# Turning the first token tiles as they land, loading the small vectors from another queue, and spacing two prefix scans

## The chip, the cores and the metric

The kernel runs on one core of one Trainium2 chip, in one launch. A core has a matmul engine (TensorE, in the profile PE, with its weight loads as PEld), VectorE (DVE), ScalarE (ACT), GpSimd (POOL) and SyncE (SP), which issues most transfers. The engines run side by side and wait for each other by semaphores. The metric is the device time of one execution in microseconds (us). An execution under the profiler gives the trace from which the rows below are taken; its clock column is the TensorE clock that was granted, as a share of 2.4 GHz.

## What is computed

One inference step of a two-layer hybrid encoder in float32, for a prompt of 1024 tokens and for 8 running streams of 16 tokens each (1152 token rows of 1024 channels in all). Cut to what the change is near to:

```
h    = rms_norm(x, norm_mix[0])              # x: 1152 x 1024
proj = h @ w_in_ab                           # 1024 -> 2560: q, fz, i_in, g, p
log_f = logaddexp(log(lb), log1p(-lb) + log_sigmoid(fz))   # decays, 4 heads x 128
b    = cumsum(log_f)                         # inside a block of the recurrence
...  # chunked linear recurrence, pooling, output projection, gated FFN with causal conv
...  # layer 2: spatial-gating MLP over 128-token chunks, gated FFN; final rms_norm
```

The vectors `norm_mix`, `norm_ffn`, `hgrn_out_gain`, `pool_scale`, `c_ln_gain` and `c_ln_bias` are small: together 69 rows of 128 numbers.

## The kernel before

**Products.** A float32 matrix is split into a high part (rounded to the matmul format) and a low part (the rest), and a product is three matmuls, high by high, high by low and low by high: `xh`, `xl` hold the activations, `wh`, `wl` the weights. The tokens are cut into three blocks of 384 (`TB`), each of three tiles of 128. A weight piece is 128x512; it is loaded into one of four `raw` buffers by SyncE's queue, scaled on GpSimd by a gain out of `vec` (`scale_weights`, L2722), rounded on ScalarE (`high`, L2111) and its low part taken on VectorE (`low`, L1345). A unit of the first projection needs two pieces, 2j and 2j + 1, and yields one row block of 128 output channels for all tokens; its results are taken from PSUM by VectorE (`scaled`, L1362) into `work`.

**The start.** The tokens lie row by row in memory, and the matmuls want channels on the partitions. SyncE loads the nine token tiles into `xtok`, three to a block (`x_tiles`, L490), all three of a block counted on one semaphore. Behind the first block it loads the 69 vector rows into `vrow` (L499), then two weight pieces, then the second block and so on. TensorE turns a block in eight groups: `turn(g)` (L777) turns one slice of 128 channels of all three tiles into one PSUM bank, six banks in rotation, so that from the seventh group on it waits until VectorE is through with the bank. ScalarE makes `xh` of each group (`x_high`, L2150), VectorE makes `xl` (`x_part`, L1389). After the fourth group TensorE also turns `vrow` (L814), ScalarE copies the result to `vec` (L2168), and GpSimd, which builds masks and constants until then, waits for `vec` before its first `scale_weights`. ScalarE's first `high` and VectorE's first `low` stand in their programs behind all eight groups of the first block. Then TensorE starts the matmuls of the first unit on the first block (`block_of`, L792), and turns the second block, then the third, between its matmuls. The squares for the norm are taken on ScalarE in between (`x_squares`, L2157). The norm follows: `spread_norm` on TensorE (L806), a root on ScalarE (L2143), a reciprocal on VectorE (L1381), and only then are the first units taken from PSUM.

**The scans.** Units 0 to 3 yield `fz`. While units 4 to 8 run on TensorE, ScalarE and VectorE make the log decays out of it, beside the weights of the coming units. The last step is a prefix sum along the tokens for each of the four heads: `tensor_tensor_scan` over 1152 elements with `resetm` as a factor that is 0 at the start of each block (`decay`, L1449). In VectorE's loop over units (`for j in range(2, BESIDE)`) iteration j does `low(2j + 1)`, `low(2j + 2)` and the three `scaled` of unit j; two scans stand behind iteration 6 and two behind iteration 7. Each engine runs its program in the written order.

Of the kernel before, what the change touches and what calls it, by code (L numbers as in the profile page):

```python
# [20 lines left out]
ACT = mybir.ActivationFunctionType  # L21
ds = bass.ds

P = 128
# [7 lines left out]
KD = D // P  # L32
# [14 lines left out]
V_MIX, V_FFN, V_OUTG, V_PSC, V_LNG, V_LNB, NVEC = 0, 16, 32, 33, 37, 53, 69  # L47
# [35 lines left out]
def build(nc, A, O):  # L83
    ctx = ExitStack()
    with ctx:  # L85
        def sem(name):
            return ctx.enter_context(nc.semaphore(name))

        x_loaded = [sem(f"x_loaded{i}") for i in range(NTB)]
        rows_loaded = sem("rows_loaded")
        raw_loaded = [sem(f"raw_loaded{i}") for i in range(RAWS)]
# [21 lines left out]
        x_turned = sem("x_turned")  # L115
# [18 lines left out]
        vec_mm = sem("vec_mm")  # L134
        vec_ready = sem("vec_ready")
# [6 lines left out]
        logf_used = sem("logf_used")  # L142
        k_ready = sem("k_ready")
        reset_ready = sem("reset_ready")
        decay_ready = sem("decay_ready")
# [114 lines left out]
        work = at("work", [P, 24, TOK], F32, W0)  # L260
# [5 lines left out]
        ident = at("ident", [P, P], F32, ID0)  # L266
# [14 lines left out]
        TURN = (1, 2, 4, 5, 6, 7)  # L281
# [188 lines left out]
        def _(sp):  # L470
# [17 lines left out]
            def x_tiles(tb):  # L488
                for t in range(3 * tb, 3 * tb + 3):
                    sp.dma_start(xtok[:, t, :], xp[:, t, :] if t < NT - 1 else xsm).then_inc(x_loaded[tb], 16)  # L490
            x_tiles(0)
            rows = [(V_MIX, A["norm_mix"].rearrange("l (k p) -> (l k) p", p=P)),
                    (V_FFN, A["norm_ffn"].rearrange("l (k p) -> (l k) p", p=P)),
                    (V_OUTG, A["hgrn_out_gain"]),
                    (V_PSC, A["pool_scale"].rearrange("l (k p) -> (l k) p", p=P)),
                    (V_LNG, A["c_ln_gain"].rearrange("l (k p) -> (l k) p", p=P)),
                    (V_LNB, A["c_ln_bias"].rearrange("l (k p) -> (l k) p", p=P))]
            for r0, src in rows:
                sp.dma_start(vrow[r0:r0 + src.shape[0], :], src).then_inc(rows_loaded, 16)  # L499

            def unit_pieces(j):
                up(wab, 2 * j, 2 * j, UNITS[j] * P)
            unit_pieces(0)
# [166 lines left out]
        def _(pe):  # L670
# [98 lines left out]
            def turn(g):  # L769

                tb, d = divmod(g, KD)
                if d == 0:
                    pe.wait_ge(x_loaded[tb], 48)
                if g >= 6:
                    pe.wait_ge(xl_ready, g - 5)
                for j in range(3):
                    mm = pe.transpose(ps[TURN[g % 6]][:, j * P:(j + 1) * P], xtok[:, 3 * tb + j, d * P:(d + 1) * P],  # L777
                                      ident[:, :])
                mm.then_inc(x_turned, 1)
# [27 lines left out]
                                   start=True, stop=True)  # L807
                mm.then_inc(norm_mm, 1)

            for g in range(KD):  # L810
                turn(g)
                if g == 3:
                    pe.wait_ge(rows_loaded, 16 * 6)
                    pe.transpose(ps[3][:, 0:NVEC], vrow[:, :], ident[0:NVEC, 0:NVEC]).then_inc(vec_mm, 1)  # L814
            block_of(0, 0, lambda k: turn(KD + k))
            pe.wait_ge(vec_ready, 1)
            block_of(1, 0, lambda k: turn(2 * KD + k))
# [523 lines left out]
        def _(dve):  # L1341
            def low(n, s):

                dve.wait_ge(w_high_ready, n + 1)
                dve.tensor_tensor(wl[:, s % 2, :], raw[:, s % RAWS, :], wh[:, s % 2, :].bitcast(F32), ALU.subtract)\  # L1345
                    .then_inc(w_low_ready, 1)
# [95 lines left out]
                dve.wait_ge(logf_ready, c + 1)  # L1442
                dve.tensor_tensor(z, f, z, ALU.subtract).then_inc(logf_used, 1)

            def decay(c):
                dve.wait_ge(logf_used, c + 1)
                dve.wait_ge(reset_ready, 3)
                for h in (2 * c, 2 * c + 1):
                    dve.tensor_tensor_scan(work[:, 20 + h, :], resetm[:, :], work[:, 20 + h, :], 0.0,  # L1449
                                           ALU.mult, ALU.add).then_inc(decay_ready, 1)  # L1450

            for j in range(2, BESIDE):
                if j > 2:
                    low(2 * j + 1, 2 * j + 1)
                if j == 6:
                    log_keys(0)
                    log_keys(1)
                low(2 * j + 2, 2 * j + 2)
                for tb in range(NTB):
                    scaled(work[:, UNITS[j], tbs(tb)], g0 + 3 * j + tb, tb, t0 + 4 * j + 2 + tb)  # L1460
                if j == 5:
                    logf(0)
                    logf(1)
                if j in (6, 7):
                    decay(j - 6)

            def evict(j):
                for tb in range(NTB):
# [636 lines left out]
        def _(act):  # L2105
# [45 lines left out]

            def x_squares(t):

                act.wait_ge(x_loaded[t // 3], 48)
                if t:
                    act.wait_ge(x_squared, t)
                act.activation(xsq[:, :], xtok[:, t, :], ACT.Square, accum_out=sst[:, t:t + 1]).then_inc(x_squared, 1)  # L2157

            def high2(q):
                act.wait_ge(w_scaled, q + 3)  # L2160
                act.activation(wh2[:, q, :], raw[:, 2 + q, :], ACT.Copy).then_inc(w_high_ready, 1)

            n0, g0, t0 = PLAN.at["ab"]
            for g in range(KD):
                x_high(g)
                if g == 3:
                    act.wait_ge(vec_mm, 1)
                    act.activation(vec[:, 0:NVEC], ps[3][:, 0:NVEC], ACT.Copy).then_inc(vec_ready, 1)  # L2168
            high(0, 0, 0)
            high(1, 1, 0)  # L2170
            for k in range(KD):
# [825 lines left out]
```

## Time and profile before

| | us |
|---|---|
| median of 3 runs (lowest, highest) | 2929.57 (2926.86, 2929.97) |
| the profiled execution, its own time | 2928.97 |
| its span, first to last instruction | 2927.3 |
| TensorE busy | 2844.0, 97% of the span |
| VectorE, GpSimd, ScalarE busy | 1503.6, 767.7, 696.9 |
| first matmul of a product starts | 14.89 |

The rows further below are read so. A row of the timeline gives the start and the length in us, engine, line, operation, what it writes and reads, and how many like instructions in a row it merges; in square brackets the time for which the engine was idle before it and what ended that. A row that merges several has the length from the first start to the last end. Consecutive instructions of an engine overlap a little, so that the step from one start to the next is shorter than a length.

### The profile page before, as it was taken

The numbers are of one execution on the slowest core, as the hardware profiler recorded it, in microseconds if no ns is written. First come the engines' busy times: TensorE is split into PE (matmuls) and PEld (weight loads), VectorE is DVE, ScalarE is ACT, GpSimd is POOL, SyncE is SP. The second block draws the span as 40 slices with busy tenths as digits, with TensorE's granted clock in tenths as the row PEclk, the third lists the DMA queues.
The fourth block names the chain that finished last, engine by engine and source line by source line (L and its number), as shares of the span: only waits on it lengthen the run. The fifth ranks groups of instructions, "written<-read, shape, count | busy, mean of one in ns | idle before, by whom it ended". The sixth has DMA issues, their size and how long they took to land. (4 is left out here: it accounts for less than half of the span.)

```text
span 2927.3 us, 44412 instructions
## 1 busy us (share of the span) xinstructions
PE 2844.0 (97%) x16227; PEld 2754.6 (94%) x16227; DVE 1503.6 (51%) x2670; ACT 696.9 (24%) x1157; POOL 767.7 (26%) x576
## 2 busy tenths in 40 slices
PE   8998989999999999999999989999999999999999
PEld 8998889999999999999788889999999999999997
DVE  4558886544444444446423865456544444444452
ACT  4414444211111111114322211214211111111123
POOL 3133334422222222223311230012422222222220
PEclk9999999999999999999999999999999999999999
DMA  4111001111111111111111111111111111111111
GB/s 141 36 35 50 19 19 43 44 41 43 39 43 39 43 39 43 36 43 49 61 44 58 33 37 43 39 43 37 47 44 39 43 39 41 42 39 43 39 55 75
DMA packets 194883, 130.72 MB, mean 45 GB/s; under 512 B 8859, under 2 KB 186724, under 8 KB 194532
## 3 DMA queue, kind: packets, MB, share of 16 engines
q1 hardware_dynamic: 194788, 129.44, 14.5%
q8 instruction: 62, 1.02, 0.1%
q14 instruction: 33, 0.27, 0.0%
HBM read 120.60 MB, written 8.81 MB: 44 GB/s over the span
## 5 line engine op out<-in xcount | busy, mean ns | idle before, releaser
L693 PE MATMUL bank<-xh,wh 128*128 128x384 f32 x2664 | 611.4, 337 | 22.0 <-DVE wl L1345 21.2
L693 PE MATMUL bank<-xl,wh 128*128 128x384 f32 x2664 | 605.5, 334 | 0.0
L693 PE MATMUL bank<-xh,wl 128*128 128x384 f32 x2664 | 605.3, 334 | 0.0
L2722 POOL TENSOR_TENSOR raw<-raw,vec 128x512 f32<-128x512 f32 x248 | 272.0, 1108 | 1224.1 <-DMA raw<-in_w_in_ffn 887.4
L2111 ACT ACTIVATE wh<-raw 128x512 fp32r<-128x512 f32 x375 | 235.8, 629 | 1463.5 <-PE bank L693 830.6
L693 PEld LDWEIGHTS bank<-xh,wh 128*128 128x128 f32 x2664 | 470.8, 188 | 37.6 <-issue 34.9
L1345 DVE TENSOR_TENSOR wl<-raw,wh 128x512 fp32r<-128x512 f32 x375 | 285.5, 762 | 396.6 <-ACT wh L2111 396.6
L693 PEld LDWEIGHTS bank<-xl,wh 128*128 128x128 f32 x2664 | 475.3, 188 | 0.0
L693 PEld LDWEIGHTS bank<-xh,wl 128*128 128x128 f32 x2664 | 475.2, 188 | 0.0
L1369 DVE TENSOR_TENSOR xs<-bank,xs 128x384 f32<-128x384 f32 (+1 forms) x648 | 320.8, 550 | 284.2 <-PE bank L718 254.9
L718 PE MATMUL bank<-yh,wh 128*128 128x384 f32 x1152 | 266.3, 339 | 7.0 <-DVE ut L1362 2.8
L718 PE MATMUL bank<-yl,wh 128*128 128x384 f32 x1152 | 265.4, 338 | 0.0
L718 PE MATMUL bank<-yh,wl 128*128 128x384 f32 x1152 | 265.2, 338 | 0.0
L718 PEld LDWEIGHTS bank<-yh,wh 128*128 128x128 f32 x1152 | 207.7, 188 | 8.4 <-DVE ut L1362 3.1
L718 PEld LDWEIGHTS bank<-yh,wl 128*128 128x128 f32 x1152 | 207.8, 188 | 0.0
L718 PEld LDWEIGHTS bank<-yl,wh 128*128 128x128 f32 x1152 | 207.6, 188 | 0.0
L2872 POOL TENSOR_TENSOR gate<-gate,cv 128x1152 f32<-128x1152 f32 x40 | 115.4, 2886 | 235.6 <-DVE xs L1369 212.3
L1362 DVE TENSOR_TENSOR gate<-bank,rstd 128x384 f32<-128x384 f32 x132 | 65.4, 550 | 195.1 <-PE bank L693 195.1
L1362 DVE TENSOR_TENSOR apad<-bank,rstd 128x384 f32<-128x384 f32 x88 | 45.0, 553 | 176.0 <-PE bank L693 176.0
L2878 POOL TENSOR_TENSOR yl<-gate,yh 128x1152 fp32r<-128x1152 f32 x40 | 114.8, 2889 | 0.0
L1833 DVE SCALAR_TENSOR_TENSOR cv<-apad,convc,cv 128x1024 f32<-128x1024 f32 x88 | 112.5, 1278 | 0.0
L2511 ACT ACTIVATE cv<-cv 128x1152 f32<-128x1152 f32 x44 | 51.3, 1166 | 223.7 <-DVE cv L1836 223.7
(319 smaller groups left out, 3460.6 us busy)
## 6 DMA issues: line engine op xcount, KB each, us to landing
raw<-in_w_in_ffn SPq DMA_DIRECT2D x176, 256.0 KB, 2.8
raw<-in_w_out_ffn SPq DMA_DIRECT2D x88, 256.0 KB, 2.6
raw<-in_w_uv_c SPq DMA_DIRECT2D x64, 256.0 KB, 2.8
raw<-in_w_in_ab SPq DMA_DIRECT2D x40, 256.0 KB, 2.9
raw<-in_w_out_c SPq DMA_DIRECT2D x32, 256.0 KB, 2.6
xtok<-in_x_prompt SPq DMA_DIRECT2D x8, 512.0 KB, 6.3
raw<-in_w_out_ab SPq DMA_DIRECT2D x16, 256.0 KB, 2.6
out_y_prompt<-otok SPq DMA_DIRECT2D x8, 512.0 KB, 2.6
```

The costliest lines, as they stand in the source:

```text
L693: mm = pe.matmul(ps[(sg + tb) % BANKS][:, 0:TB], w[:, place, k * P:(k + 1) * P], r[:, kk, tbs(tb)], start=kk == 0 and c == 0, stop=kk == K ...
L718: mm = pe.matmul(ps[(sg + g0 + tb) % BANKS][:, 0:TB], w[:, place, k * 256 + dd * P:k * 256 + (dd + 1) * P], r[:, k, tbs(tb)], start=k == 0 ...
L1345: dve.tensor_tensor(wl[:, s % 2, :], raw[:, s % RAWS, :], wh[:, s % 2, :].bitcast(F32), ALU.subtract)\
L1362: dve.tensor_tensor(dst, ps[bank % BANKS][:, 0:TB], rstd[:, tbs(tb)], ALU.mult)\
L1369: dve.tensor_tensor(xs[:, d, tbs(tb)], ps[sg % BANKS][:, 0:TB], xs[:, d, tbs(tb)], ALU.add)\
L1833: dve.scalar_tensor_tensor(outp, padp[:, j:j + SEQ], col(16 + j), outp, ALU.mult, ALU.add)\
L2111: act.activation(wh[:, s % 2, :], raw[:, s % RAWS, :], ACT.Copy).then_inc(w_high_ready, 1)
L2511: act.activation(cv[:, c, :], cv[:, c, :], ACT.Gelu).then_inc(gelu_done[l], 1)
L2722: pool.tensor_tensor(r, r, g, ALU.mult).then_inc(w_scaled, 1)
L2872: pool.tensor_tensor(gate[:, c, :], gate[:, c, :], cv[:, c, :], ALU.mult)\
L2878: pool.tensor_tensor(yl[:, c, :], gate[:, c, :], yh[:, c, :].bitcast(F32), ALU.subtract)\
```

## The change

The three tiles of the first block get a semaphore each. TensorE turns the vector rows first; then, as each tile lands, the first six channel slices of it, into the six banks; then it does groups 6 and 7 in the old way. So the six banks are filled tile by tile, and each is complete with its third tile. The vector rows are loaded by ScalarE's queue, at the head of ScalarE's program, and their copy to `vec` is the first thing that ScalarE computes. The squares of the first three tiles wait on the new semaphores. The scans are taken one by one: heads 0 and 1 behind iteration 6 as before, head 2 behind iteration 7, and head 3 in iteration 8, between its two `low`.

```diff
+        x_tile_loaded = [sem(f"x_tile_loaded{i}") for i in range(3)]
 # SyncE
-            x_tiles(0)
-            for r0, src in rows:
-                sp.dma_start(vrow[r0:r0 + src.shape[0], :], src).then_inc(rows_loaded, 16)
+            for t in range(3):
+                sp.dma_start(xtok[:, t, :], xp[:, t, :]).then_inc(x_tile_loaded[t], 16)
 # TensorE
-            for g in range(KD):
-                turn(g)
-                if g == 3:
-                    pe.wait_ge(rows_loaded, 16 * 6)
-                    pe.transpose(ps[3][:, 0:NVEC], vrow[:, :], ident[0:NVEC, 0:NVEC]).then_inc(vec_mm, 1)
+            pe.wait_ge(rows_loaded, 16 * 6)
+            pe.transpose(ps[3][:, 0:NVEC], vrow[:, :], ident[0:NVEC, 0:NVEC]).then_inc(vec_mm, 1)
+            for t in range(3):
+                pe.wait_ge(x_tile_loaded[t], 16)
+                for d in range(6):
+                    mm = pe.transpose(ps[TURN[d]][:, t * P:(t + 1) * P], xtok[:, t, d * P:(d + 1) * P], ident[:, :])
+                    if t == 2:
+                        mm.then_inc(x_turned, 1)
+            turn(6)
+            turn(7)
 # VectorE
-            def decay(c):
-                dve.wait_ge(logf_used, c + 1)
+            def decay(h):
+                dve.wait_ge(logf_used, h // 2 + 1)
...
+                if j == 8:
+                    decay(3)
...
-                if j in (6, 7):
-                    decay(j - 6)
+                if j == 6:
+                    decay(0)
+                    decay(1)
+                if j == 7:
+                    decay(2)
 # ScalarE
-                act.wait_ge(x_loaded[t // 3], 48)
+                if t < 3:
+                    act.wait_ge(x_tile_loaded[t], 16)
+                else:
+                    act.wait_ge(x_loaded[t // 3], 48)
...
+            for r0, src in rows:
+                act.dma_start(vrow[r0:r0 + src.shape[0], :], src).then_inc(rows_loaded, 16)
+            act.wait_ge(vec_mm, 1)
+            act.activation(vec[:, 0:NVEC], ps[3][:, 0:NVEC], ACT.Copy).then_inc(vec_ready, 1)
             for g in range(KD):
                 x_high(g)
-                if g == 3:
-                    act.wait_ge(vec_mm, 1)
-                    act.activation(vec[:, 0:NVEC], ps[3][:, 0:NVEC], ACT.Copy).then_inc(vec_ready, 1)
```

TensorE's program at its start, in the kernel before (`bank1` to `bank7` are the PSUM banks, `xtok_62` the token tiles, `vrow_63` the vector rows):

```order
L777 MATMUL bank1<-ident_57,xtok_62 128x128 [waits x_loaded0,ident_ready]
L777 MATMUL bank1<-ident_57,xtok_62 128x128 x2
L777 MATMUL bank2<-ident_57,xtok_62 128x128 x3
L777 MATMUL bank4<-ident_57,xtok_62 128x128 x3
L777 MATMUL bank5<-ident_57,xtok_62 128x128 x3
L814 MATMUL bank3<-ident_57,vrow_63 128x69 [waits rows_loaded]
```

The same place in the changed kernel:

```order
L804 MATMUL bank3<-ident_57,vrow_63 128x69 [waits rows_loaded,ident_ready]
L808 MATMUL bank1<-ident_57,xtok_62 128x128 [waits x_tile_loaded0]
L808 MATMUL bank2<-ident_57,xtok_62 128x128
L808 MATMUL bank4<-ident_57,xtok_62 128x128
L808 MATMUL bank5<-ident_57,xtok_62 128x128
L808 MATMUL bank6<-ident_57,xtok_62 128x128
L808 MATMUL bank7<-ident_57,xtok_62 128x128
L808 MATMUL bank1<-ident_57,xtok_62 128x128 [waits x_tile_loaded1]
```

The vector rows have moved to the front, and a bank is no longer filled in one go but once per tile.

VectorE's program around the scans, before (`work` is written from PSUM by units, `wl` is the low part of a weight piece):

```order
L1449 SCALAR_TENSOR_TENSOR work<-resetm,work 128x1152 [waits reset_ready,logf_used]
L1449 SCALAR_TENSOR_TENSOR work<-resetm,work 128x1152
L1345 TENSOR_TENSOR wl<-raw,wh 128x512 [waits w_high_ready] x2
L1362 TENSOR_TENSOR work<-bank,rstd 128x384 [waits pe_tick] x3
```

This piece stands twice in a row there; in the changed kernel the second one reads:

```order
L1446 SCALAR_TENSOR_TENSOR work<-resetm,work 128x1152 [waits reset_ready,logf_used]
L1343 TENSOR_TENSOR wl<-raw,wh 128x512 [waits w_high_ready]
L1446 SCALAR_TENSOR_TENSOR work<-resetm,work 128x1152 [waits reset_ready,logf_used]
L1343 TENSOR_TENSOR wl<-raw,wh 128x512 [waits w_high_ready]
L1360 TENSOR_TENSOR work<-bank,rstd 128x384 [waits pe_tick] x3
```

One scan has moved behind the first `wl` of the next iteration.

## Rows read from the trace of the kernel before

**Rows 1.** The page, busy time of each engine, share of the span, instructions.

```profile
PE 2844.0 (97%) x16227; PEld 2754.6 (94%) x16227; DVE 1503.6 (51%) x2670; ACT 696.9 (24%) x1157; POOL 767.7 (26%) x576
```

**Rows 2.** Waits of TensorE for `wl` in the first 200 us: total, times, longest.

```profile
PE bank L693 <- DVE wl L1345: 2.4, 3, 1.2
```

**Rows 3.** Timeline of all engines, from the first transfer to the first matmul.

```profile
0.83 1.36 SPq L490 DMA_DIRECT2D xtok<-in_x_prompt  x3
4.24 0.42 SPq L499 DMA_DIRECT2D vrow<-in_c_ln_bias  x1
8.04 2.79 PE L777 MATMUL bank<-ident,xtok 128*128 128x128 f32 x12 [8.04 <-DMA xtok<-in_x_prompt]
8.95 2.41 ACT L2150 ACTIVATE xh<-bank 128x384 fp32r<-128x384 f32 x4 [6.85 <-PE bank L777]
9.55 2.40 DVE L1389 TENSOR_TENSOR xl<-bank,xh 128x384 fp32r<-128x384 f32 x4 [9.55 <-ACT xh L2150]
10.74 2.06 PE L777 MATMUL bank<-ident,xtok 128*128 128x128 f32 x12
11.56 2.04 POOL L2722 TENSOR_TENSOR raw<-raw,vec 128x512 f32<-128x512 f32 x2 [1.78 <-ACT vec L2168]
11.63 1.82 ACT L2150 ACTIVATE xh<-bank 128x384 fp32r<-128x384 f32 x4
12.15 2.04 DVE L1389 TENSOR_TENSOR xl<-bank,xh 128x384 fp32r<-128x384 f32 x4 [0.20 <-ACT xh L2150]
13.31 1.16 ACT L2111 ACTIVATE wh<-raw 128x512 fp32r<-128x512 f32 x2
14.11 1.28 DVE L1345 TENSOR_TENSOR wl<-raw,wh 128x512 fp32r<-128x512 f32 x2
14.89 0.41 PE L792 MATMUL bank<-xh,wh 128*128 128x384 f32 x1 [2.09 <-ACT wh L2111]
```

**Rows 4.** Issue to landing: tiles 0 and 1; the sixth tile; weight piece 0.

```profile
DMA to landing us min/median/max: 3.7/4.1/4.5
DMA to landing us min/median/max: 7.6/7.6/7.6
DMA to landing us min/median/max: 4.3/4.3/4.3
```

**Rows 5.** All instructions on the token tiles: length in ns, minimum, median, maximum.

```profile
L777 PE MATMUL bank<-ident,xtok x72: 270/272/446, 8.0 to 30.5; 128*128 128x128 f32 x72
```

**Rows 6.** Stretches: busy time by engine, granted clock, DMA share, GB/s.

```profile
8.00:15.00 7.00, 4.87 (x26) 4.69 (x27) 5.08 (x10) 4.87 (x11) 3.62 (x22) 1.00 1.06 347
15.00:18.50 3.50, 3.50 (x15) 3.31 (x16) 0.95 (x2) 0.91 (x3) 2.04 (x2) 0.55 1.02 395
225.00:235.00 10.00, 5.17 (x30) 5.06 (x29) 6.83 (x13) 4.16 (x10) 0.89 (x1) 0.66 0.36 97
```

**Rows 7.** Timeline around the second unit pair: VectorE, then TensorE.

```profile
47.51 0.68 DVE L1345 TENSOR_TENSOR wl<-raw,wh 128x512 fp32r<-128x512 f32 x1
49.29 0.68 PE L693 MATMUL bank<-xh,wh 128*128 128x384 f32 x3
```

**Rows 8.** Timeline around the last scans: VectorE, ScalarE, TensorE.

```profile
127.93 5.00 DVE L1449 TENSOR_TENSOR_SCAN work<-resetm,work 128x1152 f32<-128x1152 f32 x2
132.84 0.67 DVE L1345 TENSOR_TENSOR wl<-raw,wh 128x512 fp32r<-128x512 f32 x1
126.93 0.64 ACT L2111 ACTIVATE wh<-raw 128x512 fp32r<-128x512 f32 x1 [3.63 <-PE bank L693]
133.17 0.63 ACT L2111 ACTIVATE wh<-raw 128x512 fp32r<-128x512 f32 x1 [3.59 <-PE bank L693]
131.87 0.68 PE L693 MATMUL bank<-xl,wh 128*128 128x384 f32 x3
132.39 0.68 PE L693 MATMUL bank<-xh,wl 128*128 128x384 f32 x3
133.65 0.76 PE L693 MATMUL bank<-xh,wh 128*128 128x384 f32 x3 [0.58 <-DVE wl L1345]
```

More of the change, by code:

```diff
@@ L490, in x_tiles @@
                     sp.dma_start(xtok[:, t, :], xp[:, t, :] if t < NT - 1 else xsm).then_inc(x_loaded[tb], 16)
-            x_tiles(0)
[L492 to L497, printed above, removed]
-            for r0, src in rows:
-                sp.dma_start(vrow[r0:r0 + src.shape[0], :], src).then_inc(rows_loaded, 16)
+            for t in range(3):
+                sp.dma_start(xtok[:, t, :], xp[:, t, :]).then_inc(x_tile_loaded[t], 16)
             def unit_pieces(j):
@@ L771, in turn @@
                 tb, d = divmod(g, KD)
-                if d == 0:
+                if tb and d == 0:
                     pe.wait_ge(x_loaded[tb], 48)
@@ L1443, in log_keys @@
                 dve.tensor_tensor(z, f, z, ALU.subtract).then_inc(logf_used, 1)
-            def decay(c):
-                dve.wait_ge(logf_used, c + 1)
+            def decay(h):
+                dve.wait_ge(logf_used, h // 2 + 1)
                 dve.wait_ge(reset_ready, 3)
-                for h in (2 * c, 2 * c + 1):
-                    dve.tensor_tensor_scan(work[:, 20 + h, :], resetm[:, :], work[:, 20 + h, :], 0.0,
-                                           ALU.mult, ALU.add).then_inc(decay_ready, 1)
+                dve.tensor_tensor_scan(work[:, 20 + h, :], resetm[:, :], work[:, 20 + h, :], 0.0,
+                                       ALU.mult, ALU.add).then_inc(decay_ready, 1)
             for j in range(2, BESIDE):
@@ L2161, in high2 @@
                 act.activation(wh2[:, q, :], raw[:, 2 + q, :], ACT.Copy).then_inc(w_high_ready, 1)
+            rows = [(V_MIX, A["norm_mix"].rearrange("l (k p) -> (l k) p", p=P)),
+                    (V_FFN, A["norm_ffn"].rearrange("l (k p) -> (l k) p", p=P)),
+                    (V_OUTG, A["hgrn_out_gain"]),
+                    (V_PSC, A["pool_scale"].rearrange("l (k p) -> (l k) p", p=P)),
+                    (V_LNG, A["c_ln_gain"].rearrange("l (k p) -> (l k) p", p=P)),
+                    (V_LNB, A["c_ln_bias"].rearrange("l (k p) -> (l k) p", p=P))]
+            for r0, src in rows:
+                act.dma_start(vrow[r0:r0 + src.shape[0], :], src).then_inc(rows_loaded, 16)
+            act.wait_ge(vec_mm, 1)
+            act.activation(vec[:, 0:NVEC], ps[3][:, 0:NVEC], ACT.Copy).then_inc(vec_ready, 1)
             n0, g0, t0 = PLAN.at["ab"]
```

## The prediction, made before the changed kernel was run

> **What bounds the kernel now.** I read the page first. TensorE is busy 97% of the span [rows 1]; nothing but less waiting of TensorE, or less time at a low clock, can shorten it. So the second view was TensorE's waits, in the first 200 us, where the change is: 8.0 us until the first tiles are there, 2.1 us before the first matmul [rows 3], and three waits for the low part of a weight piece that make 2.4 us [rows 2]. The third view, the timeline of the start, says who holds the first matmul. Tiles land, the turning starts at 8.04, ScalarE's first `xh` at 8.95, VectorE's first `xl` at 9.55, its eighth ends before 14.11, there its first `wl` starts, and the matmul at 14.89 is 0.78 us behind that [rows 3]. So the path to the first matmul is: third tile, first group, then VectorE's eight `xl` and one `wl`. GpSimd's wait for `vec` until 11.56 and ScalarE's `wh` at 13.31 lie beside it. Behind that TensorE's next wait is the first of those three for `wl`, behind 100 us, so what is gained at 14.89 can go through to the end, if the side chains follow. The sum is made against the profiled execution's own time, 2928.97 us, 0.6 below the median of the three runs and well inside their spread of 3.1 (2926.86 to 2929.97).
>
> **The start: what it removes.** The twelve first transposes take 2.79 us; less the 0.45 of one [rows 5] that is (2.79 - 0.45) / 11 = 0.213 us a piece [rows 3]. A group is three of them, 0.64 us, and for the first four groups this sets the pace: ScalarE's four take 2.41. In the second half ScalarE goes by its own pace, (13.31 - 11.63) / 4 = 0.42, and VectorE by (14.11 - 12.15) / 4 = 0.49 us [rows 3]. Under the change, the first two tiles are turned ahead; each of the six banks then is one transpose from ready, and the pace is VectorE's 0.49. If tile 2 can be turned when it lands, at 8.04, the first bank is ready after one transpose, not three: 2 x 0.213 = 0.43 earlier. ScalarE then starts at 8.52, VectorE at 9.12, eight steps of 0.49 end at 13.04, against 14.11: the most that this part can bring is 1.07 us.
>
> Groups 6 and 7 don't stop this. They wait for VectorE's first and second `xl` (done near 9.7 and 10.2) and take 0.64 + 0.24 us each, so they are there at 10.6 and 11.2, before ScalarE wants them at 11.0 and 11.5. The weights come along: GpSimd is through with its constants at 11.56 - 1.78 = 9.78 [rows 3], piece 0, issued at 4.71, lands after 4.3 us at 9.0 [rows 4], so a scaled piece is there at 9.78 + 1.02 = 10.8 and ScalarE's `wh` can start at 12.
>
> **The start: what it adds.** The turning of the vectors now stands ahead of everything on TensorE, and `rows_loaded` with it: behind that wait are all 18 first transposes, behind these ScalarE and VectorE. With R the time at which the six vector loads have landed, tile 2 can be turned at R + 0.23 (the vectors' transpose) + 12 x 0.213 = R + 2.8, or at 8.04 if that is later. Tiles 0 and 1 are no bound: issued at 0.83 and 1.26 they land after 3.7 and 4.5 us, at 4.5 and 5.8 [rows 4]. So nothing is lost up to R = 5.24, from there every microsecond of R is one of the first matmul, and at R = 6.31 the gain is gone.
>
> R isn't in the trace. On SyncE the first vector issue follows the tiles, whose three end at 0.83 + 1.36 = 2.2, and the sixth starts at 4.24, 2.0 us later [rows 3]; at the head of ScalarE's program the sixth would start at 0.83 + 2.0 = 2.84. From issue to landing the nearest rows are 3.7 us for the first tile and 4.3 for a weight piece between others [rows 4], both far larger than 8 KB. At 347 GB/s [rows 6] the 512 KB of a tile take 1.5 us of that, which leaves 2.2. So R lies between 2.84 + 2.2 = 5.0 and 2.84 + 4.3 = 7.1. I take R = 5.6, 2.8 us from issue, since the rows are small but the engines are busy with tiles at that time. The bounds give 1.07 us of gain and 7.14 - 6.31 = 0.8 us of loss; R = 5.6 gives 1.07 - 0.36 = 0.71.
>
> The Trainium skill, page "DMA: Bandwidth & Descriptors", section "Queues, rings and completion order", says that each DMA engine takes turns between the queues of different issuers, a packet at a time. By that the vectors would not stand behind three tiles, and R would be at the lower end; in this trace all loads come from SyncE, so no row shows two queues side by side.
>
> With 0.71 the first matmul starts at 14.18. Its next need is the second block: `turn` at 14.6, while the sixth tile, issued at 6.73, lands 7.6 us later at 14.33 [rows 4]. The queue moves data all through that time, so issuing earlier by the vectors' 2.4 us brings nothing, but there is just no wait either. SyncE's weight pieces and tiles come in the same order. ScalarE spends about 2.4 us on issues, from 0.8 on, where it otherwise waits until 8.95: nothing.
>
> **Does the gain last?** The first place where the side chain could take it back is unit 2 at 49.29. Its `wl` starts at 47.51 and is there at 48.2 [rows 7]: 1.1 us of slack, more than 0.71, and the chain ahead of it (squares, root, reciprocals) is fed by the same turning, so it comes earlier too. Later stalls hang on TensorE's own ticks and move with it.
>
> **The scans.** Two scans take 5.00 us, 2.5 each [rows 8]. Piece 17's `wl` waited for the second one and started at 132.84, though its high part was done at 126.93 + 0.64 = 127.6. TensorE's groups of three follow each other by 132.39 - 131.87 = 0.52; the one behind 132.39 began at 133.65, not at 132.91, so 0.74 us were lost [rows 8]. With one scan ahead only, `wl` runs from 130.4 to 131.1; TensorE wants it at 132.91, 1.8 us later. The moved scan then takes 131.1 to 133.6, and piece 18's `wl` can start when ScalarE is through, at 133.17 + 0.63 = 133.8, as before: covered, with 0.2 us to spare, and TensorE wants that piece only a half unit later, twelve groups of 0.52 behind 132.91, at 139. Gain 0.74. Of this no bound is far: 0 if something else holds the piece, 0.8 if the slower first group behind the wait (0.60 for 0.52) goes too. The other two stalls [rows 2] stay.
>
> **Sum.** 0.71 + 0.74 = 1.45: 2928.97 - 1.45 = 2927.5 us.
>
> **The clock.** After the first matmul the clock fell. 15.00 to 18.50 has 0.55 [rows 6], so about 3.2 us at 1.2 GHz; the 7 us ahead of it held 4.87 us of TensorE work and the wait of 2.1. Half of 3.2 us is what it costs: 1.6. The change moves the idle stretch (now from 11.4 to 14.2, with shorter ones between the tiles), so this can go either way, by up to 1.6. The low stretch near 230 lasted (1 - 0.66) x 10 / 0.5 = 6.8 us [rows 6], so one of twice the length does occur. I put it at zero in the sum.
>
> The step between transposes falls within the turning: 0.213 us in the first twelve, (2.06 - 0.27) / 11 = 0.16 in the second [rows 3, 5]. The Trainium skill, page "TensorE: Matmul & The Clock Gate", part on the PE-mode transpose, says that transposes don't count as work that raises the clock. By that no turning would help the matmuls to 2.4 GHz, early or late; the trace has them speed up with nothing but turning done, so here it did.
>
> **The rivals.**
> - The vectors land late (R = 7.1). For it: the wait stands ahead of all turning, and loads between others took 4.3 us. Against: they are small and issued at once with the tiles. Loss 0.8 at the start, 0.74 gained at the scans: 2929.0, no change.
> - Slower: TensorE enters the first matmuls at 1.2 GHz and stays there for 6.8 us. Place: the stretch behind the first matmul. For it: the turning is torn into pieces by the tiles, and the idle stretch before the matmul grows from 2.1 to 2.8 us. Against: before, the clock fell as well. Price: 3.6 us more of low clock, 1.8 us; with the gain of 1.45 it comes out at 2929.3. It decides from 2.9 us of extra low clock on.
> - Only half of it works. Either VectorE's chain of squares, roots and reciprocals doesn't move and takes the start's gain at 49.29 (2928.2), or piece 17 is late for another reason and the stall at 133 stays (2928.3). For it: ScalarE takes the squares of nine tiles between its `xh`. Against: the slack of 1.1 and of 1.8 us.
> - Better: the clock doesn't fall at all behind the first matmul, 1.6 us more. The slack at 49.29 then is used up, and about 1.4 of it come through: 2926.1.
>
> **How the numbers follow.** Forecast 0.48; vectors late 0.14; slow clock 0.15; half of it 0.11; better 0.12. The forecast's own range is 2926.4 to 2928.6, from the bounds of R. The other cases lie in 2926.1 to 2929.3. The three runs of one kernel stand 3.1 apart, so a median may be off by one or so: 2924.9 to 2930.3 for the range. A change that a measurement of this kernel can tell is 0.2%, 5.9 us; no case comes near it, on either side. I leave 0.04 for faster and 0.04 for slower, 0.92 for within.
>
> **What would show it.** Right: the vectors' transpose starts by 5.8, the first `xh` near 8.9 or sooner, four of them in 1.8 us rather than 2.4, the first matmul near 14.2; no wait for `wl` near 132, two such waits left. Wrong: a first transpose after 6.5; the first matmul after 14.9; a wait at 49; a clock row under 0.6 for 15 to 22; a median above 2930.3 or below 2924.9.

## The result and the profile after

The changed kernel takes 2934.74 us (median of 20 runs, 2931.22 to 2939.01); before takes 2930.06 in the same study (20 runs, 2926.86 to 2933.99). The ratio is 1.0015, 95% interval 1.0009 to 1.0022: slower by 4.7 us, where 1.5 us less was forecast. The profiled execution took 2938.55 us; it is one of the longest of its kernel, so the text reads from it where things happen, and takes how much from many runs. Where a mean difference is given below with ±, it is between all runs of a kernel and the 135 of before, over the five studies, with one standard error: the change comes to +4.1 ± 0.4 us (31 runs). Two slow runs, 4.7 ms of before and 12.6 ms of vec_later_sp, are left out everywhere.

The page of the changed kernel, its first lines; TensorE has the same 16227 matmuls and 7.2 us more busy time [rows 1]. The page of before counts 44412 instructions, two fewer; the experiments come back to that.

```profile
span 2936.8 us, 44414 instructions
PE 2851.2 (97%) x16227; PEld 2760.9 (94%) x16227; DVE 1502.5 (51%) x2670; ACT 696.1 (24%) x1157; POOL 765.4 (26%) x576
```

Waits of TensorE in the first 300 us (what was waited for: us in total, times, longest). The three waits for `wl` of [rows 2] have become two, and 9.2 us pass before anything is turned, where the first tiles were waited for 8.0 us [rows 3]:

```profile
PE bank L804 <- DMA vrow<-in_c_ln_bias: 9.2, 1, 9.2
...
PE bank L785 <- issue: 3.3, 1, 3.3
...
PE bank L686 <- DVE wl L1343: 1.9, 2, 1.3
```

The timeline of its start, to be laid beside [rows 3]:

```profile
0.82 1.35 SPq L493 DMA_DIRECT2D xtok<-in_x_prompt  x3
...
3.04 1.35 ACTq L2175 DMA_DIRECT2D vrow<-in_c_ln_bias  x1
...
9.19 0.35 PE L804 MATMUL bank<-ident,vrow 69*128 69x69 f32 x1 [9.19 <-DMA vrow<-in_c_ln_bias]
...
9.34 4.04 PE L808 MATMUL bank<-ident,xtok 128*128 128x128 f32 x18
...
12.35 3.17 ACT L2152 ACTIVATE xh<-bank 128x384 fp32r<-128x384 f32 x8 [2.54 <-PE bank L808]
12.95 3.81 DVE L1387 TENSOR_TENSOR xl<-bank,xh 128x384 fp32r<-128x384 f32 x8 [12.95 <-ACT xh L2152]
...
16.68 1.69 DVE L1343 TENSOR_TENSOR wl<-raw,wh 128x512 fp32r<-128x512 f32 x2
...
17.86 0.66 PE L785 MATMUL bank<-xh,wh 128*128 128x384 f32 x1 [3.29 <-issue]
```

The last of the six vector loads was issued at 3.04 and has landed only at 9.19. All 18 transposes stand behind it and run without a gap, so by then all three tiles are there and nothing is turned "as it lands". Tile 2 landed 7.0 us after its issue at 1.7, so at 8.7; in before it took 6.1 us. The first matmul is at 17.86, 2.97 us later than before. It takes 0.66 us, and 0.52 those behind it, against 0.41 and 0.34 at full clock (the rows of warm_count below): TensorE is at 1.2 GHz here. Two windows (stretch, length, busy us of PE, PEld, DVE, ACT and POOL with instructions, granted clock, DMA share, GB/s) show it; the same 7 us had 0.76 before:

```profile
15.00:22.00 7.00, 4.14 (x15) 3.98 (x16) 3.96 (x8) 2.59 (x7) 2.70 (x3) 0.64 0.70 251
...
15.00:25.00 10.00, 7.14 (x31) 6.75 (x32) 5.19 (x10) 4.72 (x11) 5.64 (x8) 0.66 0.49 176
```

0.66 over the 10 us is (1 - 0.66) x 10 / 0.5 = 6.8 us at 1.2 GHz, twice what stood there before. The scans, on VectorE:

```profile
131.79 2.55 DVE L1446 TENSOR_TENSOR_SCAN work<-resetm,work 128x1152 f32<-128x1152 f32 x1
134.26 0.67 DVE L1343 TENSOR_TENSOR wl<-raw,wh 128x512 fp32r<-128x512 f32 x1
134.84 2.55 DVE L1446 TENSOR_TENSOR_SCAN work<-resetm,work 128x1152 f32<-128x1152 f32 x1
```

They are apart, and TensorE's groups follow each other by 0.52 all through: the stall of [rows 8] is gone. So the profile has one part that does the opposite of its forecast, and one that does what was forecast.

### The profile page after: what moved, and what is told of

It reads as the page before. It is cut to its first block and busy times, and to the rows that moved or that the text cites. A ratio compares the mean times of both kernels' runs of the same rounds, so it can differ in the third digit from the quotient of the medians.

```text
span 2936.8 us, 44414 instructions
## 1 busy us (share of the span) xinstructions
PE 2851.2 (97%) x16227; PEld 2760.9 (94%) x16227; DVE 1502.5 (51%) x2670; ACT 696.1 (24%) x1157; POOL 765.4 (26%) x576
```

## The experiments

**The halves.** start_only is the changed kernel with the scans pairwise as before; scans_only is before with the scans apart:

```diff
# start_only, against the changed kernel     # scans_only is the same edit the other way, on before
-                if j == 8: decay(3)
-                if j == 6: decay(0); decay(1)
-                if j == 7: decay(2)
+                if j in (6, 7): decay(j - 6)      # two scans each
```

> The changed kernel with the scans two by two as before, so the start alone. Theory A: the vectors land near 9.2, the first matmul starts near 17.9 (3.0 later than before), 4.5 to 5.5 us slower than before in the median, of which 3.0 are the wait and the rest low clock behind it. Rival B (part of the loss comes from the scans' new places): no more than 4 us slower, and the changed kernel would be at least as slow as this one.

> The kernel before with the scans taken one by one as in the change, its start untouched. Theory A (the two halves of the change act apart; the loss is made by the wait for the vectors ahead of all turning, the scans gain): two waits for wl instead of three in the first 200 us, the third unit half behind 132 starts 0.8 us earlier, 0.7 to 0.8 us faster than before. Rival B (the scans' gain is given back further on, by the chain of exponents and levels behind 140): the wait is gone too, but TensorE's first level matmul stands where it stood and the time is that of before, 0.0.

> The kernel before with the scans one by one, again, to halve the scatter. Theory A: 0.7 to 0.8 us faster than before over both sets together. Rival B: no gain (0.0), or, if the first set was right on both counts, slightly slower.

start_only: 2932.61 us, 1.0011 (1.0002 to 1.0020), +2.9 ± 0.6, less than the 4.5 to 5.5 that was expected of it. Vectors turned at 8.40, first matmul at 17.30. scans_only: 2930.45, 1.0001 (0.9992 to 1.0010), and in a second study 2931.69, 1.0006 (0.9997 to 1.0015); its two sets of 11 lie at +0.3 and +1.6, together at +1.0 ± 0.4, where 0.7 to 0.8 less was expected. The halves add up: 2.9 + 1.0 = 3.9 of 4.1. The start is most of the loss. And the scans, whose stall is gone in the trace, gain nothing in time; that is taken up further down.

**The changed kernel again**, in another study.

> The changed kernel once more, beside the kernel before on one chip, to see how far the landing of the vectors scatters. Theory A (the vectors' transfers share the DMA engines with tiles that fill them, so their landing lies near 8 to 9 us whatever the execution): vectors' transpose between 8.2 and 9.3, first matmul 3 us after where the kernel before has it, 3 to 5 us slower in the median. Rival E (9.2 was a rare late landing, caused by the last issue on ScalarE that took 1.35 us): transpose before 7, hardly slower than before.

2934.13 us, 1.0013 (1.0004 to 1.0022); vectors turned at 8.52, first matmul at 17.19. Late vectors are no accident of one execution, and not the work of the sixth issue, which took 1.35 us in the first profile (the row at 3.04) and 0.47 here.

**Why do the vectors land so late?** rows_alone holds the tiles back until they are there; vec_first lets SyncE issue them ahead of the tiles; act_rows_only is before with nothing but the vector loads moved to ScalarE's queue.

```diff
# rows_alone, against the changed kernel
+            sp.wait_ge(rows_loaded, 16 * 6)
             for t in range(3):
                 sp.dma_start(xtok[:, t, :], xp[:, t, :]).then_inc(x_tile_loaded[t], 16)
# vec_first, against the changed kernel (ScalarE's six loads are gone)
+            for r0, src in rows:
+                sp.dma_start(vrow[r0:r0 + src.shape[0], :], src).then_inc(rows_loaded, 16)
             for t in range(3):
```

> The changed kernel, but SyncE starts the tiles only when the six vector loads have landed, so these run with the DMA engines to themselves. Theory A (contention with the tiles makes the landing late): the vectors' transpose starts at 5.0 to 5.5, that is 2 to 2.5 us behind the sixth issue. Rival F (six small loads are slow by themselves, by issue and by fixed latency): it starts at 7 or later with nothing beside them. The kernel as a whole is several microseconds later; only the landing is asked for.

> The changed kernel with the six vector loads issued by SyncE ahead of the tiles rather than by ScalarE beside them; turned first as in the change. Theory A: alone in the queue for 2 us the vectors land at 5 to 6, the tiles come 2.0 to 2.4 us later than before (the third near 10), the first transpose of tile 2 near 10; first matmul at about 10.0 + 0.45 + 0.6 + 3.9 + 0.8 = 15.8, 1 to 1.5 us later than before and earlier than in the change; 1 to 2 us slower than before in the median. Rival G (order in the queue doesn't matter, tiles still land near 8): first matmul at 14 or sooner, faster than before by 1 us or more.

> The kernel before with the vectors' loads on ScalarE's queue and nothing else changed: they are turned behind the fourth group as before. Theory A: at 10.6 they have landed anyway, so no wait there; first matmul near 14.4 to 14.9 as before. Rival D (a second queue beside the tiles' slows tiles and weights): the first transpose starts 0.5 us or more later than 8.0, or GpSimd waits for the weight piece.

TensorE in rows_alone, and then in vec_first:

```profile
4.67 0.35 PE L805 MATMUL bank<-ident,vrow 69*128 69x69 f32 x1 [4.67 <-DMA vrow<-in_c_ln_bias]
8.39 2.82 PE L809 MATMUL bank<-ident,xtok 128*128 128x128 f32 x12 [3.38 <-DMA xtok<-in_x_prompt]
```

```profile
4.60 0.35 PE L812 MATMUL bank<-ident,vrow 69*128 69x69 f32 x1 [4.60 <-DMA vrow<-in_c_ln_bias]
...
10.25 1.54 PE L816 MATMUL bank<-ident,xtok 128*128 128x128 f32 x6 [0.30 <-DMA xtok<-in_x_prompt]
...
15.87 0.66 PE L793 MATMUL bank<-xh,wh 128*128 128x384 f32 x1 [2.88 <-ACT wh L2121]
```

With nothing of SyncE in flight the same six loads of the same queue are there at 4.67, 1.7 us behind the last issue at 2.94; beside tiles and weight pieces it takes 5.4 to 6.2. On SyncE's queue they are there at 4.60 if they stand ahead of the tiles. So it isn't the queue, nor the size, but what SyncE has in flight beside them; tiles and weight pieces were not tried apart. vec_first pays for it with the third tile, turned at 10.25: first matmul 15.87, as expected, and 2932.93 us, 1.0012 (1.0003 to 1.0021), 2.7 ± 0.7 above before where 1 to 2 was expected. rows_alone took 2932.01 in its one run. act_rows_only, where the turning of the vectors stands behind the fourth group, turns them at 10.77 without a wait (when they landed no row shows), has its first matmul at 14.69 and took 2929.33 in one run: no cost shows where nothing waits for them. The Trainium skill, page "DMA: Bandwidth & Descriptors", says in the section "Issuing engines are not separate DMA queues" that loads of all issuers run on the same 16 DMA engines and interleave. The two kernels agree with it: the vectors are there at 4.67 us on one queue and 4.60 on the other, against 8.4 to 9.2 with tiles and pieces in flight.

**The wait put where it holds nobody.** vec_later turns the vectors behind the 18 transposes; ScalarE copies them behind its fourth `xh`. vec_later_sp also gives the loads back to SyncE, behind the tiles.

```diff
# vec_later, against the changed kernel
-            pe.wait_ge(rows_loaded, 16 * 6)
-            pe.transpose(ps[3][:, 0:NVEC], vrow[:, :], ident[0:NVEC, 0:NVEC]).then_inc(vec_mm, 1)
             for t in range(3):
...
+            pe.wait_ge(rows_loaded, 16 * 6)
+            pe.transpose(ps[3][:, 0:NVEC], vrow[:, :], ident[0:NVEC, 0:NVEC]).then_inc(vec_mm, 1)
             turn(6)
```

> The changed kernel with the turning of the vectors moved behind the eighteen first transposes, and their copy on ScalarE behind its fourth xh as before; the loads stay on ScalarE's queue. Theory A (only the wait's place is wrong): first transpose near 5 to 6 us, first xh near 8.5 to 9, first matmul near 13.8 to 14.0, one microsecond earlier than before; 1.5 to 2 us faster than before, and 6 us faster than the change. Rival C (the tiles one by one are themselves harmful, since each tile lands later when vectors and weights crowd the queues, or since torn turning leaves the clock low): first matmul at 15 or later, or a low stretch twice as long behind it; not faster than before.

> The changed kernel with the vectors turned behind the eighteen transposes, again, on one chip with the two kernels built on it. Theory A: 1.5 us faster than before over both sets, of which the first set showed nothing. Rival I (most of the start's gain of 1.7 us at the first matmul is taken by low clock, 0.5 to 1 us of it left by unit 2, and clock stretches later on move the time by more than that): within 0.5 us of before.

> As the one with the vectors turned later, but their loads issued by SyncE behind the first three tiles, as before; so of the start only the turning tile by tile is left. Theory A: vectors are there by 9.5, when the eighteen transposes end, and the time equals that of the kernel with the loads on ScalarE's queue within 0.5 us. Rival D (the queue matters: loads on ScalarE's queue hold up tile 2 or the weights): this one is faster by 0.5 us or more, with the third tile landing near 8.0, not 8.8.

TensorE in vec_later:

```profile
4.77 4.35 PE L806 MATMUL bank<-ident,xtok 128*128 128x128 f32 x18 [4.77 <-DMA xtok<-in_x_prompt]
8.94 0.24 PE L810 MATMUL bank<-ident,vrow 69*128 69x69 f32 x1
...
13.22 0.66 PE L785 MATMUL bank<-xh,wh 128*128 128x384 f32 x1 [2.88 <-ACT wh L2113]
```

Now the tiles are turned as they land, from 4.77 on, and the first matmul is at 13.22, 1.67 ahead of before. But it starts at 1.2 GHz (0.66 us). vec_later takes 2930.91 us, 1.0001 (0.9992 to 1.0009), and again 2929.39, 0.9998 (0.9989 to 1.0007); +0.2 ± 0.5 over 22 runs, so the 1.5 to 2 us below before that were expected did not come. It is 3.9 ± 0.6 below the changed kernel: the place of that one wait accounts for all of the start's loss. vec_later_sp comes to 1.0003 (0.9994 to 1.0012): the vectors ahead of the second block make its turning wait 1.15 us for a tile at 15.55. Its vectors, on SyncE's queue behind the tiles, were waited for until 8.65, 4.4 us behind their last issue: late on this queue too.

**The waits for `wl`, and the clock at the start.** spread is vec_later with VectorE's work beside units 4 to 8 laid out more evenly. Its expectation says that never two long operations stand ahead of one `wl`; the edit leaves two in two places, `logf(1)` and `log_keys(0)` for one, but none of them stalls TensorE. warm adds transposes of the identity into a bank that is overwritten later; nothing reads them.

```diff
# spread, VectorE's loop, against vec_later
                 # ahead of low(2j+2)            # behind the scaled() of unit j
-  j=5                                           logf(0) logf(1)
-  j=6           log_keys(0) log_keys(1)         decay(0) decay(1)
-  j=7                                           decay(2)
-  j=8           decay(3)
+  j=5                                           logf(0)
+  j=6           logf(1) log_keys(0)             decay(0)
+  j=7           decay(1), log_keys(1) behind it decay(2)
+  j=8           decay(3)
# warm, TensorE, against spread
+            def warm(n):
+                for _ in range(n):
+                    pe.transpose(ps[0][:, 0:P], ident[:, :], ident[:, :])
+            warm(20)                    # ahead of the first tile
...
             turn(7)
+            warm(16)
```

> The kernel with the vectors turned later, and the VectorE work between units 5 and 8 spread further: one log step, one key step or one scan between two low parts, never two, so that no low part waits for more than one of them. Theory A (the stalls of units 6, 7 and 8 are all made by what stands ahead of a low part on VectorE): no wait for wl in the first 135 us, first matmul of unit 9 (the one beside the recurrence) 1.8 us earlier after its own first matmul than in the kernel with the vectors turned later, and 1.5 to 2 us faster than that one in the median. Rival B (gains around 130 are given back behind 140): the waits are gone, the time equals that of the other kernel within 0.5 us.

> The spread kernel, with transposes of the identity whose result nobody reads put into TensorE's idle time at the start: 20 ahead of the first tile, 16 behind group 7. Theory C (idle TensorE ahead of the first matmul is what leaves the clock at 1.2 GHz for 3 to 7 us behind it): granted clock above 0.9 from 13 to 19 us, the unit at 48 begins 1.5 to 2.5 us sooner than without, 1 to 2 us faster than the spread kernel. Rival H (transposes don't raise the clock): low stretch of 3.4 or 6.8 us behind the first matmul as before, same time within 0.5 us.

spread: 2928.80, 0.9994 (0.9985 to 1.0003); no wait for `wl` is left in the first 137 us, and it is 1.5 ± 0.9 below vec_later in the same study. warm: 2926.92, 0.9987 (0.9978 to 0.9996), 1.7 ± 0.7 below spread. Its first matmul is at 13.38 and takes 0.41, spread's at 13.39 takes 0.66. The clock column is no witness here: it reads 1.00 for 15 to 22 us in both, though spread's matmuls still take 0.67 and 0.52 until 17 us. The time from the first matmul to unit 2 is one: 34.2 us in spread, 32.5 in warm and in warm_count further down. scans_only_2 and act_rows_only, which have the old start, take 32.4 in their profiles without such transposes, so two profiles alone would not settle it; the mean of the runs speaks for it, by a little more than twice its error.

The first matmuls in spread, and then in warm:

```profile
13.39 0.66 PE L785 MATMUL bank<-xh,wh 128*128 128x384 f32 x1 [2.35 <-ACT wh L2111]
...
15.77 0.52 PE L785 MATMUL bank<-xh,wl 128*128 128x384 f32 x1
```

```profile
13.38 0.41 PE L785 MATMUL bank<-xh,wh 128*128 128x384 f32 x1 [1.13 <-ACT wh L2117]
```

**Why do scans that stall nobody gain nothing?** The traces of all kernels so far with the scans apart show TensorE waiting 0.6 to 1.1 us longer for `wl` in the second feed-forward, 1600 us and more behind the scans, where not one instruction differs: 10.2 to 10.5 us against 9.4 (before, start_only) and 9.6 (act_rows_only). Before, and then scans_only, 1735 to 2850 us:

```profile
PE bank L693 <- DVE wl L1345: 9.4, 20, 0.7
```

```profile
PE bank L693 <- DVE wl L1345: 10.5, 20, 0.7
```

In VectorE's loop there one place differs, the second tap of the convolution. Before, and then scans_only:

```profile
2220.11 0.34 DVE L1836 SCALAR_TENSOR_TENSOR cv<-apad,convc,cv 128x128 f32<-128x128 f32 x1
2220.37 1.28 DVE L1833 SCALAR_TENSOR_TENSOR cv<-apad,convc,cv 128x1024 f32<-128x1024 f32 x1
```

```profile
2219.88 0.34 DVE L1840 SCALAR_TENSOR_TENSOR cv<-apad,convc,cv 128x128 f32<-128x128 f32 x1
2220.21 1.28 DVE L1837 SCALAR_TENSOR_TENSOR cv<-apad,convc,cv 128x1024 f32<-128x1024 f32 x1
```

The step is 0.26 us in the one and 0.33 in the other. Of the 22 such steps all are 0.26 before; in scans_only one in each of the loop's nine rounds is longer, 0.58 the first time and 0.32 or 0.33 the next eight, which sums to 0.32 + 8 x 0.065 = 0.84 us. The first:

```profile
2142.87 0.35 DVE L1840 SCALAR_TENSOR_TENSOR cv<-apad,convc,cv 128x128 f32<-128x128 f32 x1
2143.45 1.29 DVE L1837 SCALAR_TENSOR_TENSOR cv<-apad,convc,cv 128x1024 f32<-128x1024 f32 x1 [0.24 <-DVE cv L1840]
```

What the split does to the program ahead of the loop is two instructions more: two scans that were called in a pair now bring their own two waits, and the page counts 44414 instructions against 44412, so that of two waits one stands as an instruction of its own. So the loop's code stands two instructions further on. Three kernels take this apart from the order of the scans, and a fourth uses it:

```diff
# scans_count, against scans_only; warm_count is the same edit on warm
+                if h % 2 == 0:
                     dve.wait_ge(logf_used, h // 2 + 1)
                     dve.wait_ge(reset_ready, 3)
# waits_only, against before (scans pairwise, in their old places)
                 for h in (2 * c, 2 * c + 1):
+                    if h % 2:
+                        dve.wait_ge(logf_used, c + 1)
+                        dve.wait_ge(reset_ready, 3)
# waits_more, against waits_only (the wait for logf_used now stands last)
+                        for _ in range(4):
                             dve.wait_ge(reset_ready, 3)
```

> Before, with the four scans apart as in the change, but the two waits stand only ahead of the first scan of each pair, so that VectorE's program has as many instructions as before; nothing at the start is changed. Theory 'place of the loop code' (the two wait instructions that the split adds ahead of the feed-forward loops shift their code): TensorE's waits for VectorE's wl in 1735 to 2850 us are back at 9.4 us in 20 waits (10.5 with the waits), the wait near 133 us is gone as in scans_only, and the time is 0.8 us (0.3 to 1.3) below before: 2929.4 where before is at 2930.3. Rival 'split itself' (the new order of the scans costs it by some path of data): 10.4 us again, and the time is 0.3 to 1.2 us above before.

> Before, scans pairwise in their old places, but the second scan of each pair also has the two waits that are met already: two instructions more on VectorE ahead of the feed-forward loops, nothing else. Theory 'place of the loop code': the wl waits in 1735 to 2850 us rise from 9.4 to 10.4 us in 20 waits, the wait near 133 us stays (0.58 at TensorE's row), and the time is 1.2 us (0.7 to 1.7) above before: 2931.5 at 2930.3. Rival 'split itself': 9.4 us, and the time is that of before within 0.2 us.

> As waits_only, with five met waits instead of two ahead of the second scan of each pair: eight instructions more than before instead of two. Theory 'place of the loop code': the wl waits in 1735 to 2850 us change with the place, so they are another figure than before's 9.4, but not four times the 1.0 us that two instructions add: between 9 and 12 us. If instead each added instruction costs (a count, not a place), 13 us or more. Rival 'split itself': 9.4 us.

> The kernel warm (vectors later, VectorE's work spread, dummy transposes at the start, whose results nothing reads) with the two waits of the scans of odd heads left out, as their pair's first scan has waited for the same. Theory 'place of the loop code': wl waits in 1735 to 2850 us 9.3 to 9.4 us instead of warm's 10.3, and the time 1.2 us (0.6 to 1.8) below warm: 2925.5 where before is at 2930.3, ratio 0.9984. Rival 'split itself': 10.3 us and the time of warm, 2926.7, ratio 0.9988.

The same row in scans_count, waits_only, waits_more and warm_count:

```profile
PE bank L693 <- DVE wl L1345: 9.4, 20, 0.7
```

```profile
PE bank L693 <- DVE wl L1345: 10.3, 20, 0.7
```

```profile
PE bank L693 <- DVE wl L1345: 9.4, 20, 0.7
```

```profile
PE bank L686 <- DVE wl L1349: 9.5, 20, 0.7
```

Split without added instructions: 9.4. Added instructions without split: 10.3, and the stall at 133 us stays (0.57). With the waits of waits_more: 9.4 again, with the step between the taps back at 0.26 (2222.29 to 2222.55). Its expectation counts eight added instructions; the page shows four, 44416 against 44412, since its repeated waits went in pairs into one instruction. In waits_only the step is 0.33:

```profile
2223.06 0.35 DVE L1839 SCALAR_TENSOR_TENSOR cv<-apad,convc,cv 128x128 f32<-128x128 f32 x1
2223.39 1.28 DVE L1836 SCALAR_TENSOR_TENSOR cv<-apad,convc,cv 128x1024 f32<-128x1024 f32 x1
```

All 18 profiles fall in line: the twelve with two instructions more have the 0.58 and eight longer steps, and the six others, waits_more among them in one profile, do not. So the waiting depends on how many instructions stand ahead of the loop, not on the order of the scans, and not in proportion to the count. That is shown. Another loop of VectorE tells the same, off TensorE's path: between 1771 and 1775 us VectorE is idle for 1.44 us ahead of a group of `xs` in before and scans_count, and for 1.09 in scans_only, waits_only and waits_more. That VectorE has to load a piece of a loop's code just there, more of it the first time, is a reading that fits the 0.58 and the eight 0.33; no row shows the loading itself. In time: scans_count 2928.99, 0.9994 (0.9985 to 1.0003), -1.7 ± 0.5; waits_only 2932.94, 1.0008 (0.9999 to 1.0017), +2.3 ± 0.3; waits_more 2931.12 in one run. Both means lie about 1 us further from before than was expected. The two instructions thus cost 2.3 ± 0.3 (waits_only over before) or 2.6 ± 0.6 (scans_only over scans_count), and the row finds 1.0 of it. The rest, 1.3 ± 0.3 or 1.6 ± 0.6, is not explained.

warm_count is the best kernel of this study: 2925.60 us, 0.9983 (0.9974 to 0.9992), -5.2 ± 0.5. Its start:

```profile
1.61 4.01 PE L805 MATMUL bank<-ident 128*128 128x128 f32 x20 [1.61 <-POOL ident L2757]
5.46 1.65 PE L811 MATMUL bank<-ident,xtok 128*128 128x128 f32 x12
8.21 0.87 PE L811 MATMUL bank<-ident,xtok 128*128 128x128 f32 x6 [1.11 <-DMA xtok<-in_x_prompt]
9.57 0.28 PE L815 MATMUL bank<-ident,vrow 69*128 69x69 f32 x1 [0.48 <-DMA vrow<-in_c_ln_bias]
...
10.64 1.91 PE L805 MATMUL bank<-ident 128*128 128x128 f32 x16
13.68 0.41 PE L785 MATMUL bank<-xh,wh 128*128 128x384 f32 x1 [1.13 <-ACT wh L2118]
13.93 0.34 PE L785 MATMUL bank<-xl,wh 128*128 128x384 f32 x1
```

## Why the prediction was wrong

**What failed: the size of R**, the time at which the vector loads have landed. The prediction took 5.6 and bounded it by 5.0 and 7.1; it was 9.19, 8.52 and 8.40 in three profiles. The rule that it built on R held: from R = 6.31 on, each microsecond is lost. 14.89 + (R - 6.31) is 17.77, 17.10 and 16.98; measured were 17.86, 17.19 and 17.30. So the mechanism was that of its first rival, at a price it didn't allow: 2.3 to 3.0 us instead of 0.8. The upper bound was the error. It was taken from a load of 4.3 us from issue to landing, although tile 2, issued at 1.8 and so the nearest in time, took 6.1 us in the trace of before, and [rows 4] has one of 7.6. 2.84 + 6.1 = 8.9 is about where the vectors came in; with 2.84 + 7.6 the bound would have been 10.4, and the loss up to 4.1. Issue to landing of tiles 1 and 2, before:

```profile
DMA to landing us min/median/max: 4.5/5.3/6.1
```

"The rows are small" was the reason for the low value, and rows_alone shows that this reason is right only where nothing of SyncE is in flight: 4.67.

**By the rule of the skill.** The Trainium skill, page "DMA: Bandwidth & Descriptors", section "Queues, rings and completion order", says that queues take turns on each DMA engine, and the prediction drew from it that R would be at the lower end. With tiles beside them the small loads landed at 8.4 to 9.2, so a queue of their own didn't protect them; the trace does not agree with what was drawn from that rule.

**The early turning.** Its most was put at 1.07 us. vec_later, which has the vectors out of the way, is 1.67 ahead of before, but before's 14.89 is one profile: in the seven with the old start the first matmul stands at 14.13 to 14.93, 14.6 in the mean, and in the six with the vectors turned later at 13.11 to 13.68, 13.3 in the mean. So the gain is 1.3 us. This part was sound and never came into play in the changed kernel. "Does the gain last?" was answered too well, though: at unit 2 the seven stand at 48.4 in the mean and the four of the six that have no extra transposes at 48.2. The low clock took the rest, as the paragraph on the clock shows.

**The gain at the scans** was put at 0.74 with a bound of 0.8 for the stall and was there in the profiles with the scans apart: TensorE goes through 133 us without a wait, and from the start of unit 2 to that of unit 9 (L848 or L850) it takes 89.8 to 89.9 us in scans_only, scans_count, after_again and the changed kernel, against 90.7 in before, start_only, waits_only and waits_more. scans_count's mean is 1.7 ± 0.5 below before. What the prediction did not have is the cost of two added wait instructions in a loop 1600 us further on. It named 0 as the lower bound of this part; scans_only came out at +1.0 ± 0.4. No row of before could have told this; the bound of 0 had no row either.

**The clock** was put at zero, ± 1.6. In the profiled execution 6.8 us at 1.2 GHz stand around the first matmuls, as in the rival "slow clock", and unit 2 starts at 53.14, 3.85 behind [rows 7], of which 2.97 is the later start. But after_again has 0.76 for 15 to 22 us, like before, with all of the loss. So the low clock adds to one execution and does not carry the result. What a low stretch costs was put at 1.6; from the first matmul to unit 2 before takes 34.4 us and the four profiles at full clock there 32.4 to 32.5, so it is 1.9 or 2.0. The four with the vectors later and no extra transposes take 34.2 to 36.0 (the last, vec_later_sp, with 1.15 us of waiting for a tile), 34.9 in the mean, where the seven with the old start take 33.8; that is where their earlier first matmul went. Of the transposes the prediction said, against the Trainium skill, page "TensorE: Matmul & The Clock Gate", part on the PE-mode transpose, that they raise the clock. The runs bear the prediction out, and not the page: behind nothing but transposes the first matmuls run at 0.41 and 0.34 us in before, and with 36 more transposes in warm and warm_count also up to unit 2, where vec_later starts at 0.66 and 0.52.

**The sum.** Forecast -0.71 at the start and -0.74 at the scans; measured +2.9 ± 0.6 and +1.0 ± 0.4. Of the signs of being wrong in "What would show it" three came: a first transpose after 6.5, a first matmul after 14.9, a median above 2930.3. A clock under 0.6 for 15 to 22 did not (0.64), nor a wait at 49.

## What to carry to other kernels

A wait that is moved to the head of an engine's program is priced by the latest landing that its load can have among the other loads of that moment, not by its size: take the slowest row of the trace for such a load as the bound, and put the wait behind all work that does not need it. Where TensorE would idle ahead of its first matmuls, try transposes that nobody needs: here they kept its clock up in two profiles of two and brought 1.7 ± 0.7 us. Judge the start by several profiles, for the first matmul of one and the same start moved by 0.8 us from one to the next. And when an edit adds or drops even a wait or two ahead of a loop that is run many times, look at a wait inside that loop before and after, for a change of 1 us there can undo a gain elsewhere.

## What the runs showed of the hardware

- Six small loads (69 rows of 128 numbers) on ScalarE's queue landed 1.7 us after the last issue with nothing of SyncE in flight, and 5.4 to 6.2 us after it beside three 512 KB tiles and weight pieces of SyncE's queue (the changed kernel twice, start_only).
- Two more instructions (met waits) ahead of a loop of VectorE made one step between two taps in each round 0.33 us long instead of 0.26, and 0.58 in the first round, and TensorE's waits 10.3 us instead of 9.4; four more left both at 0.26 and 9.4.
- Transposes after an idle stretch step by (4.04 - 0.27) / 17 = 0.22 us in the changed kernel and by (1.91 - 0.27) / 15 = 0.11 in warm_count's second batch, yet the clock column reads 1.00 for 8 to 15 us in both; in spread it reads 1.00 also for 15 to 17 us, where the matmuls take 0.67 and 0.52. Around the first matmuls the step between like instructions says more than the column.
